# Delta-rule items of TensorE share a place between dense pieces, eleven places a tile instead of fifteen

## The reference

```
A   = where(strict, einsum(kb, k) * decay, 0)            # kb = k * beta, per chunk
rhs = concat([v * beta, kb * exp(gc)])
sol = triangular_solve(I + A, rhs, lower, unit_diagonal) # -> u_val, w_k
qk  = where(causal, einsum(q, k) * decay, 0)
def step(S, chunk):                                       # over the chunks, in order
    v_new = u - w_k @ S
    o     = q_dec @ S + qk @ v_new
    S     = S * g_last + k_dec^T @ v_new
o_a = rmsnorm(o) * silu(gate)                             # beside it: u * (w_s @ v + b_s)
```

## Time and profile before

| | us |
|---|---|
| median of 3 runs | 2584.57 (2582.55 to 2587.33) |
| the profiled execution | 2588.94 |
| its span | 2587.2, mean granted clock 0.991 |
| PE busy | 2518.5 (97%) |
| DVE busy | 1368.5 (53%) |
| ACT busy | 1114.1 (43%) |
| POOL busy | 281.6 (11%) |

### The profile page before, as it was taken

One profiled execution on the slowest core, in us unless ns is written; L12 is line 12 of the kernel. 1 busy time (PEld: TensorE's weight loads), 2 busy tenths in 40 slices (PEclk: granted clock), 3 DMA queues, 4 the chain that ended last, 5 costly groups with the idle time before them and its releaser, 6 DMA issues.

```text
span 2587.2 us, 40036 instructions
## 1 busy us (share of the span) xinstructions
PE 2518.5 (97%) x16667; PEld 2253.1 (87%) x16667; DVE 1368.5 (53%) x2223; ACT 1114.1 (43%) x1869; POOL 281.6 (11%) x453
## 2 busy tenths in 40 slices
PE   8998989999999999999999999999999999999998
PEld 7778888787787798899999989998877988999998
DVE  4746764655555565434454475536654466443344
ACT  6554446454554354333333345433332345323324
POOL 4121111100001001111101001122111000000000
PEclk9999999999999999999999999999999999999999
DMA  7554335533334356544434245555445343333232
GB/s 207 159 162 111 107 109 138 162 89 96 112 93 118 93 171 189 152 124 117 113 94 116 86 119 162 173 150 144 122 130 155 115 144 97 98 107 113 84 90 84
DMA packets 370420, 323.62 MB, mean 125 GB/s; under 512 B 13113, under 2 KB 340851, under 8 KB 370240
## 3 DMA queue, kind: packets, MB, share of 16 engines
q1 hardware_dynamic: 336224, 207.91, 27.9%
q0 software_dynamic: 34016, 113.15, 14.9%
HBM read 263.43 MB, written 57.58 MB: 124 GB/s over the span
## 4 chain that ended last, share of the span: by engine, by line
PE 83%; DVE 6%; ACT 5%; DMA 3%; issue 2%; POOL 1%; DVEq 0%; ACTq 0%; POOLq 0%
PE dense L630 76%; PE mixer L630 6%; ACT arena L1264 1%; DVE wlo L1785 1%; ACT whi L1264 1%; DVE arena L2019 1%; PE mixer L696 0%; DVE arena L2021 0%; DVE hf L1926 0%; ACT relu L1264 0%; DMA arena<-xrow 0%; ACT L1264 0%; DMA wst<-in_w_in_even_dram 0%; ACT L1269 0%; DMA arena<-mrow 0%
## 5 line engine op out<-in xcount | busy, mean ns | idle before, releaser
L630 PE MATMUL dense<-hhi,whi 128*128 128x272 f32 (+1 forms) x3072 | 847.2, 330 | 22.0 <-DVE wlo L1785 16.9
L630 PE MATMUL dense<-hhi,wlo 128*128 128x272 f32 (+1 forms) x3072 | 826.9, 324 | 0.0
L630 PE MATMUL dense<-hlo,whi 128*128 128x272 f32 (+1 forms) x3072 | 825.4, 323 | 0.0
L1785 DVE TENSOR_TENSOR wlo<-wst,whi 128x1024 fp32r<-128x1024 f32 x384 | 469.6, 1223 | 230.9 <-ACT whi L1264 229.9
L1264 ACT ACTIVATE whi<-wst 128x1024 fp32r<-128x1024 f32 x384 | 403.8, 1052 | 419.9 <-PE dense L630 406.4
L630 PEld LDWEIGHTS dense<-hhi,whi 128*128 128x128 f32 x3072 | 517.4, 189 | 77.2 <-DVE wlo L1785 22.5
L630 PEld LDWEIGHTS dense<-hhi,wlo 128*128 128x128 f32 x3072 | 515.3, 190 | 41.7
L630 PEld LDWEIGHTS dense<-hlo,whi 128*128 128x128 f32 x3072 | 517.5, 189 | 38.1 <-issue 0.7
L630 PE MATMUL dense<-h1hi,whi 128*128 128x272 f32 (+1 forms) x1536 | 423.8, 330 | 11.1 <-DVE wlo L1785 5.8
L630 PE MATMUL dense<-h1hi,wlo 128*128 128x272 f32 (+1 forms) x1536 | 414.6, 324 | 0.0
L630 PE MATMUL dense<-h1lo,whi 128*128 128x272 f32 (+1 forms) x1536 | 412.7, 323 | 0.0
(11 more groups left out here) (397 smaller groups left out, 1808.0 us busy)
## 6 DMA issues: line engine op xcount, KB each, us to landing
wst<-in_w_ff_dram SPq DMA_DIRECT2D x256, 512.0 KB, 3.9
wst<-in_w_in_even_dram SPq DMA_DIRECT2D x48, 512.0 KB, 4.2
wst<-in_w_in_odd_dram SPq DMA_DIRECT2D x48, 512.0 KB, 3.9
proj<-ffh POOLq DMA_DIRECT2D x48, 272.0 KB, 2.5
proj<-ffh POOLq DMA_DIRECT2D x48, 256.0 KB, 2.3
arena<-proj POOLq DMA_DIRECT2D x24, 512.0 KB, 4.8
out_dram<-arena POOLq DMA_DIRECT2D x17, 512.0 KB, 5.0
wst<-in_w_out_even_dram SPq DMA_DIRECT2D x16, 512.0 KB, 4.1
```

The source lines that it names most:

```text
L630: return pe.matmul(out, lhsT, rhs, start=start, stop=stop)
L1785: TT(wlo[:, u % 2, :], wst[:, u % 2, :], whi[:, u % 2, :].bitcast(F32), ALU.subtract)\
```

## The change

`mix` now takes a list of items as one place. `gdn` uses that: for each tile, `dec`, `kk` and `kT` share a place with a rest before and behind it (in tile 0, `sum` with `dec`, and `kk` with `kT`); `vn` and `zw` share one; `sum` of the next tile and `oT` of this share one, behind a rest. `kT` and `zw` no longer have a place, and with the added rests an inner tile has 28 places in all instead of 29, of which 11 hold work of PE instead of 15. `schedule` puts the cut between the part of the second list that goes beside the output projection and the rest at 13 instead of 14. No item is added, removed or changed; only how many dense pieces lie between them differs.

```diff
     def mix(self, rows, side):
         done = 0
+        side = [place if isinstance(place, list) else [place] for place in side]
         for i, row in enumerate(rows):
             self.order += row
             upto = (i + 1) * len(side) // len(rows)
-            self.order += side[done:upto]
+            self.order += sum(side[done:upto], [])
             done = upto
-        self.order += side[done:]
+        self.order += sum(side[done:], [])
...
     def gdn(tiles):
+
         out = []
+        step = lambda t, *names: [("g", t, s, 0) for s in names]
         for i, t in enumerate(tiles):
+            more = i + 1 < len(tiles)
             if i == 0:
-                out += [("gx", t), ("g", t, "act", 0)] + [("g", t, "gv", 0)] * (t >= 4) + [("g", t, "sum", 0)]
-            out += [("g", t, s, 0) for s in ("dec", "kk", "kT")] + [("rest",)]
-            out.append(("g", t, "vT", 0))
-            more = i + 1 < len(tiles)
+                out += [("gx", t)] + step(t, "act") + step(t, "gv") * (t >= 4)
+                out += [step(t, "sum", "dec"), step(t, "kk", "kT"), ("rest",)]
+            else:
+                out += [("rest",), step(t, "dec", "kk", "kT"), ("rest",)]
+            out += step(t, "vT")
             if more:
                 out.append(("gx", t + 1))
-            out += [("rest",)] * 1 + [("g", t, s, 0) for s in ("b1", "b2", "b3")] + [("rest",)] * 5
-            out.append(("g", t, "b4", 0))
+            out += [("rest",)] + step(t, "b1", "b2", "b3") + [("rest",)] * 5 + step(t, "b4")
             for q in range(LB, LEVELS):
                 out += [("g", t, "la", q), ("g", t, "lb", q)]
                 if q == 4 and more:
-                    out.append(("g", t + 1, "act", 0))
+                    out += step(t + 1, "act")
                 if q == 5 and more and t + 1 >= 4:
-                    out.append(("g", t + 1, "gv", 0))
+                    out += step(t + 1, "gv")
             if i == 0:
                 out += [("gx2", t), ("rest",), ("rest",)]
-            out += [("g", t, s, 0) for s in ("vn", "zw", "o")]
-            out.append(("g", t + 1, "sum", 0) if more else ("rest",))
-            out.append(("g", t, "oT", 0))
+            out += [step(t, "vn", "zw")] + step(t, "o") + [("rest",)]
+            out.append((step(t + 1, "sum") if more else []) + step(t, "oT"))
             if more:
                 out.append(("gx2", t + 1))
         return out
...
-        self.mix(rows, side[:14])
+        self.mix(rows, side[:13])
...
-        self.mix(rows[4:-8], side[14:])
+        self.mix(rows[4:-8], side[13:])
```

## The result

The changed kernel takes 2592.1 us (median of 11 runs, 2589.24 to 2594.17) where the kernel before takes 2584.57 (11 runs, 2582.39 to 2588.82). The ratio is 1.0024, 95% interval 1.0016 to 1.0032: 6 us slower, between 4 and 8 (the two medians by themselves are 7.5 apart). Forecast were 8 us faster. The profiled executions differ by less, 2592.49 and 2588.94, spans 2590.8 and 2587.2. Part of that is the profile of before: against the profiles of the other kernels, further down, it lies high in the input-projection stage and in the part that nobody touched.

A forecast was written before the change was run, and what follows sets the result against it. PE, busy 97% of the span, was taken to bound the kernel, leaving its stalls and the lower clock behind them. Terms 0 - 4.0 - 3.2 + 0.4 + 0.3 - 1.8 = -8.3 us gave a median of 2576.3, range 2569 to 2588.

The forecast's parts named there:

- A place by itself: PE's own cost of each of the 32 places taken out: 0 us, bounds 0 and -0.3.
- Tile 5: Beside the first FF: `h1lo` and `wlo` come ahead of `b2` and `b3`, the stall goes; -4.0 us, bounds -4.1 and 0.
- tile 6 to 7: Beside the FF: `act` ahead of the evacuation removes a stall, less a new one at `gv`; -3.2 us, bounds -4.3 and 0.
- The price of 1.1 us for `gv`: Tile 7, beside the FF: `gv`'s earlier table load ahead of a `whi` makes a new stall of about 1.1 us.
- Tile 4's head: `kT` of tile 4 now stands with `kk` ahead of a unit's `wlo`: +0.3 us, bounds 0 and +1.
- The sample tile: Items about two pieces earlier shorten waits at the two `gs u` and small ones: -1.8 us, bounds -3.2 and +1.
- The small waits at 830 to 838 us: Sample tile: these waits shorten as its items come earlier, -0.5 us.
- Tiles 0 to 3: Beside the input projection: `dec`, `kk`, `kT` in one place; gains and losses by tile sum to +0.4 us, bounds -4 and +8.
- One of its own signs of being wrong: The forecast is wrong if the input projection's window grows by over 3 us.
- The bunch on the chain, the other side: Rival: `A` behind ACT's whole block costs tiles 1 to 3 and 5 to 7; +5.5 us, 2590; chance 0.17.
- The stalls move and do not go: Rival: two new stalls of 2 us with lower clock give back 7.4 us, about 2584; chance 0.28.
- The rule on table loads: Skill's 2.66 us a switch would make `gv`'s stall about 3.9 us, forecast some 3 higher; the prediction went by the rows.

The follow-up runs named there:

- e8_28: Kernel before with one rest fewer in each of tiles 4 to 7 and no place shared; ratio 1.0005.
- e10_split: Kernel before with new lists for tiles 4 to 7 behind the head, `sum` and `oT` apart, second `gs u` one place later than the change; 2578.03 us, ratio 0.9972.
- e12_gv: e10_split with `gv` of tile 7 put behind `la` of level 6; 2577.43 us, ratio 0.9966 against the kernel before.
- e3_head: Changed kernel with `sum` and `dec` of tile 4 in places of their own and the cut at 14; ratio 1.0005 against the kernel before.
- e6_u1: Kernel before with only the second `gs u` of the sample tile one place (two pieces) earlier; ratio 1.0006.
- e4_again: Kernel before with nothing changed, run again; ratio 0.9998.
- e7_kin: Kernel before with only `dec`, `kk`, `kT` in one place in tiles 0 to 3 (tile 0: `sum` with `dec`, `kk` with `kT`); ratio 1.0009.
- e1_in: Kernel before with the new lists in tiles 0 to 3 alone; ratio 1.0010.
- e9_dec: e1_in with `dec` one place earlier, ahead of `kk` and `kT` (`sum` and `dec` apart in tile 0); ratio 1.0008 against the kernel before.
- e11_head: Kernel before with only `sum` and `dec` of tile 4 in one place and the cut at 13; ratio 1.0014.
- e13_vT_late: e1_in with `vT` one piece later again, as in the kernel before; ratio 1.0009 against the kernel before.
- e14_vT_early: Kernel before with `vT` one piece earlier in tiles 0, 1 and 3; ratio 1.0006.

## Why the prediction was wrong

- **A place by itself: 0.** Right. In e8_28 and e10_split, with more places that hold work of PE than the change has, nothing is lost that a row doesn't explain.
- **Tile 5: -4.0; tile 6 to 7: -3.2.** Right in mechanism and nearly in size: in the profiles -3.5 between 590 and 700 us and -3.7 between 700 and 820. That it is so near for tile 5 is in part luck: the forecast was read from one profile, and in five of the nine with this stall the clock does not fall behind it; against those the gain is about 2. The price of 1.1 us for `gv` was right too, and e12_gv took it away. The bound of 0 for the first was too careful, the rows had all that was needed. Missed beside them: 1.3 us at `sum` with `oT` of tile 5, balanced in part by 0.7 where `kT` left the FF.
- **Tile 4's head: +0.3. This step failed**, by 4.1 us. The prediction took the shift of `kT` for the whole effect, and that one costs nothing (e3_head, 0.0). The lists had it: `act`, `gv` and `sum` two pieces later. I had priced every item that moved earlier by what stands ahead of it and let those that moved later pass as harmless. It was the largest single mistake, and without it the change would have been near zero (e3_head, 1.0005).
- **The sample tile: -1.8. This step failed**, by 4.7 us. "A piece earlier leaves the `wlo` more" came out at the first update, 0.8 us. At the second it did not: the update passed the evacuation that ACT's `sq` and the next `whi` hang on, and the wait grew by 0.8 (in e6_u1, a piece earlier still, the same order gains 0.6). And the DMAs released by that instruction were not followed, which cost 2.0. The small waits at 830 to 838 us, taken at -0.5, gave no time back either. The upper bound of +1 came from DVE alone.
- **Tiles 0 to 3: +0.4; this term was mis-sized**: +3.5 by the means. By tile the forecast was 0, -1.2, +0.2 and +1.4 and the means have +2.1, +0.3, +0.9 and +0.2. Its list has no term for `vT`, whose wait makes up for what tile 1 gains at `b4`; tile 0, taken as 0, cost most; tile 3's 1.4 did not come. The bounds of -4 and +8 held it, but the +8 is said to be worked out further on and is not. One of its own signs of being wrong was met: the input projection's window grew by 3.3 us.
- **The rivals.** "The bunch on the chain, the other side" had a chance of 0.17 and got the sign. Its mechanism was not what happened: no block on ACT passed the cover in tiles 5 to 7, and its own part, 1.4 more in each of tiles 1 to 3, is not there either: these three cost 1.4 together. "The stalls move and do not go" is what happened in e8_28; it speaks of 28 places for 29, where it is 28 for 30. The bounds of the terms, added, reach +10, or 2594.6, beyond the result; the range was cut short at the slow side, where the two terms with the least work in them stood.
- **The rule on table loads** (2.66 us a switch; in the Trainium skill it stands in "ScalarE: Activation LUTs", "What ACT_TABLE_LOAD costs", and not on the page that the prediction names) made no difference to the outcome: with it the wait at `gv` would have been 3.9 us, and it was 1.1.

## What to carry to other kernels

When a schedule is a list spread evenly over the work of the bounding engine, taking a place out moves everything behind it by a piece or two, and what that does is decided by single pieces; compare the positions of all items, those that move later too, and follow for each what it releases on other engines, its DMAs first. A store that is issued early is not free: here a weight transfer that is issued just behind 2.25 MB of other transfers, four stores first, lands after 10.7 us, though it is on another queue. And a change that is a bundle should be taken apart on the chip: of this one two parts cost 4.4 and 2.9 us by the profile, and without these and the bunch in tiles 0 to 3 what is left gains 0.2 to 0.3%.

## What the runs showed of the hardware

- The same stall can have two prices. PE waits 1.9 us on `wlo` at tile 5 in every kernel that leaves that place as before. In four profiles (before, e4_again, e6_u1, e7_kin) the granted clock in the 3.6 us behind it is 0.53 or 0.54, in five (e1_in, e9_dec, e11_head, e13_vT_late, e14_vT_early) it is 1.00, here e11_head's, against the earlier trace rows:

```profile
603.90:607.50 3.60, 3.60 (x16) 1.00 0.66 164
```

  The two kinds differ by 1.6 us of time in that stretch. So a stall of 2 us costs 2.1 or about 3.7, and which of them is not settled by the stall; a profile shows only one. The stall of 2.7 us at tile 7 has two prices as well: the clock is down behind it in all nine, but in e1_in and e14_vT_early for about twice as long, and they lose 1.5 us more there. (Over the 6.8 us from where the clock falls it is 0.50 in e1_in and 0.75 in the kernel before.) What makes the one or the other is not shown.
- A weight transfer of 512 KB takes about 4 us to land as a rule here (median of the page), 5.6 when it is issued just behind one transfer of POOL's, and 10.7 when it is issued behind five (2.25 MB); its packets hardly move before those of the five are through, though they are on another queue.
- A table load of ScalarE takes 1.28 us and nothing beside: the next activation starts 0.02 us later.
